# Experts' weight stream reordered: the next expert's first up pair is projected between an expert's last pair and its down projection

## The reference, cut to what matters

```python
def swiglu(t, w1, w3, w2):
    return (jax.nn.silu(t @ w1) * (t @ w3)) @ w2

def moe_swiglu(h, w_router, b_router, w1, w3, w2):
    shp = h.shape
    t = h.reshape(-1, shp[-1])
    logits = (t @ w_router).astype(jnp.float32) + b_router.astype(jnp.float32)
    top_v, top_i = lax.top_k(logits, TOP_K)          # TOP_K = 2
    top_w = jax.nn.softmax(top_v, axis=-1)
    combine = jnp.sum(jax.nn.one_hot(top_i, N_EXPERTS, dtype=jnp.float32) * top_w[..., None], axis=1)
    y = None
    for e in range(N_EXPERTS):                       # 8
        ye = combine[:, e:e + 1] * swiglu(t, w1[e], w3[e], w2[e]).astype(jnp.float32)
        y = ye if y is None else y + ye
    return y.astype(h.dtype).reshape(shp)
```

## Time and profile before

| | |
|---|---|
| Median of three runs | 2604.79 us |
| Profiled execution | 2603.11 us |
| Its span | 2601.3 us |
| Mean granted TensorE clock | 0.962 |
| TensorE matmuls busy | 2434.9 us, 94% of the span |
| VectorE, ScalarE, GpSimd busy | 1768.2, 1260.9, 525.7 us |
| HBM read | 500.33 MB |
| Experts' stage | about 1785 to 2584 us of the span |

### The profile page before, as it was taken

The page is one execution under the profiler, slowest core; times in us unless marked ns, Lnnn a source line. Parts: engine busy times, 40 slices in busy tenths (PEclk is TensorE's granted clock), DMA queues, the critical chain, the costliest instruction groups (busy, mean ns, idle before and its releaser), DMA issues.

```text
span 2601.3 us, 36325 instructions
## 1 busy us (share of the span) xinstructions
PE 2434.9 (94%) x13800; PEld 2037.3 (78%) x13824; DVE 1768.2 (68%) x1887; ACT 1260.9 (48%) x1457; POOL 525.7 (20%) x407
## 2 busy tenths in 40 slices
PE   7999999999999988779999989889999999999997
PEld 5668998769997855658889967577788888887886
DVE  6566865456865766558645357657888888888886
ACT  5444344444433455332222134536667677677674
POOL 1003531003522000031002520002142232222321
PEclk9989999999999998789999989888999999999999
DMA  5424554454552310025555323026989889889894
GB/s 195 161 82 155 179 185 159 175 196 151 189 195 77 114 41 1 33 88 193 192 193 192 130 73 115 9 84 228 347 321 365 336 336 352 335 343 357 324 363 181
DMA packets 71469, 503.73 MB, mean 194 GB/s; under 512 B 8193, under 2 KB 8705, under 8 KB 11265
## 3 DMA queue, kind: packets, MB, share of 16 engines
q1 hardware_dynamic: 70128, 496.75, 52.0%
q0 software_dynamic: 1168, 4.66, 0.5%
HBM read 500.33 MB, written 1.05 MB: 193 GB/s over the span
## 4 chain that ended last, share of the span: by engine, by line
PE 83%; DVE 10%; ACT 4%; issue 2%; POOL 1%; DMA 0%; DVEq 0%; ACTq 0%; SPq 0%; PEldq 0%
PE ps L418 80%; DVE ring_r L2103 1%; DVE h L2081 1%; PE ps L458 1%; POOL h_r L1350 1%; DVE h L2079 1%; DVE areaA L2073 1%; PE ps L1174 1%; ACT ring_hi L1467 1%; DVE h L2083 1%; ACT h L1546 1%; DVE areaB L2595 1%; DVE temp L2166 0%; DVE h L2680 0%; PE ps L561 0%
## 5 line engine op out<-in xcount | busy, mean ns | idle before, releaser
L1467 ACT ACTIVATE ring_hi<-ring 128x2048 fp32r<-128x2048 f32 x427 | 807.5, 1893 | 576.6 <-PE ps L418 351.1
L2852 DVE TENSOR_TENSOR ring_r<-ring,ring_hi 128x2048 fp32r<-128x2048 f32 x264 | 628.9, 2389 | 114.9 <-ACT ring_hi L1467 113.9
L418 PE MATMUL ps<-ring_hi,extra_r 128*128 128x512 f32 (+2 forms) x1808 | 610.3, 394 | 32.0 <-DVE ring_r L2103 18.4
L2103 DVE TENSOR_TENSOR ring_r<-ring,ring_hi 128x2048 fp32r<-128x2048 f32 (+3 forms) x163 | 384.6, 2359 | 197.7 <-ACT ring_hi L1467 182.9
L418 PE MATMUL ps<-extra_r,ring_hi 128*128 128x256 f32 (+1 forms) x1432 | 462.5, 323 | 21.7 <-POOL h_r L1350 20.2
L418 PE MATMUL ps<-extra_r,ring_r 128*128 128x256 f32 (+1 forms) x1432 | 458.0, 320 | 0.0
L418 PE MATMUL ps<-h_r,ring_hi 128*128 128x256 f32 (+2 forms) x1400 | 445.7, 318 | 0.0
L418 PEld LDWEIGHTS ps<-ring_hi,extra_r 128*128 128x128 f32 x1808 | 343.7, 190 | 109.1 <-DVE ring_r L2103 21.4
L418 PE MATMUL ps<-ring_r,extra_r 128*128 128x512 f32 (+2 forms) x1104 | 427.0, 387 | 0.0
L418 PEld LDWEIGHTS ps<-extra_r,ring_hi 128*128 128x128 f32 x1432 | 272.8, 190 | 45.4 <-POOL h_r L1350 23.4
L418 PEld LDWEIGHTS ps<-extra_r,ring_r 128*128 128x128 f32 x1432 | 272.7, 190 | 19.0
(11 more groups left out here) (356 smaller groups left out, 3257.0 us busy)
## 6 DMA issues: line engine op xcount, KB each, us to landing
ring<-in_experts SPq DMA_DIRECT2D x264, 1024.0 KB, 4.9
ring<-in_stream SPq DMA_DIRECT2D x202, 1024.0 KB, 4.8
ring<-in_stream SPq DMA_DIRECT2D x6, 512.0 KB, 3.6
ring<-in_stream SPq DMA_DIRECT2D x2, 576.0 KB, 3.7
res<-in_xT SPq DMA_DIRECT2D x1, 1024.0 KB, 6.0
res<-in_ctxT POOLq DMA_DIRECT2D x1, 1024.0 KB, 7.4
h<-in_consts POOLq DMA_DIRECT2D x2, 512.0 KB, 4.8
areaB<-in_cond_rows POOLq DMA_DIRECT2D x1, 1024.0 KB, 6.4
```

What stands on the lines that cost most here:

```text
L418: return pe.matmul(o, l, r, start=start, stop=stop, skip_group_check=True)
L1467: return act.activation(dst, src, ACT.Copy)
L2103: L.tell(TTN(ring_lo[:, s, 0:n], ring[:, s, 0:n], ring_hi[:, j % HIS, 0:n].bitcast(F32), ALU.subtract), "weights_lo")
L2852: TTN(ring_lo[:, s, :], ring[:, s, :], ring_hi[:, j % HIS, :].bitcast(F32), ALU.subtract).then_inc(sig("weights_lo"), 1)
```

## The change: what it does

The stream's order becomes a table, `EXPERT_ORDER`: after chunk 21 of an expert come chunks 0 and 1 of the next, then its own chunks 22 to 32, then chunk 2 of the next. TensorE's program, the order of loads, the layout of the weights in HBM and the walks of ScalarE and VectorE follow that table. The two halves of the expert's output (banks 3 and 2) are taken out by separate instructions of 512 columns: bank 3 first, then the split of a chunk, then bank 2. The waits before the down projection move inside its first chunk, whose matmuls into bank 2 go first. The waits of ScalarE and of the loads on TensorE's progress use one semaphore, `moe_used`, in place of four. VectorE's copy of gathered tokens comes before the split of its position, not after. The held-back split at position 21 stays only for the last expert.

The order table and TensorE's program:

```diff
@@ -113,6 +113,13 @@
         "n2_0": [(hf, q) for q in range(4) for hf in range(2)], "n1_1": ONE + [(1, q) for q in range(4)],
         "n2_1": ONE, "final": ONE}
 ROUTED = 80
+EXPERT_ORDER = [(0, 0), (0, 1)]
+for _e in range(NE):
+    EXPERT_ORDER += [(_e, _c) for _c in range(2, KF)]
+    if _e < NE - 1:
+        EXPERT_ORDER += [(_e + 1, 0), (_e + 1, 1)]
+    EXPERT_ORDER += [(_e, _c) for _c in range(KF, CPE)]
+EXPERT_AT = {x: _n for _n, x in enumerate(EXPERT_ORDER)}
 MIXED = {"even": 0, "odd": 2, "mix0": 4, "mix1": 8}
...
@@ -1225,28 +1224,48 @@
     pe.wait_ge(sig("xexp_hi"), i * (2 * NE) + 1)
     gather_share(0, 0)
     pe.wait_ge(sig("wcur"), i * (2 * NE) + 2)
+    def up(e, j):
+
+        n = e * NP + j
+        b = n % 2
+        if j == 0:
+            pe.wait_ge(sig("xexp_hi"), i * (2 * NE) + (2 * e + 2))
+            pe.wait_ge(sig("xexp"), i * (2 * NE) + (2 * e + 2))
+        pe.wait_ge(sig("moe_val"), i * (NE * NP) + (n + 1))
+        for half in range(2):
+            v = expert_weights(i, EXPERT_AT[e, 2 * j + half], "p (k c) -> p k c", k=4)
+            for k4 in range(4):
+                k = 4 * half + k4
+                m = mm3(ps[:, b, :], lambda s: xexp[s][:, e % 2, k, :], lambda s: v[s][:, k4, :],
+                        k == 0, k == KD - 1)
+            m.then_inc(sig("moe_used"), 1)
+
+    def down(e):
+
+        for c in range(KF // 2):
+            v = expert_weights(i, EXPERT_AT[e, KF + c], "p (k c) -> p k c", k=2)
+            pe.wait_ge(sig("moe_hidden"), i * (NE * NP) + (e * NP + c + 3))
+            steps = [(kk, a) for a in range(2) for kk in range(2)] if c == 0 else [
+                (kk, a) for kk in range(2) for a in range(2)]
+            for x, (kk, a) in enumerate(steps):
+                kt = 2 * c + kk
+                if c == 0 and x == 2:
+                    pe.wait_ge(sig("moe_turned"), i * (NE * NP) + (e * NP + NP + 1))
+                m = mm3(ps[:, 2 + a, :], lambda s: hid[s][:, kt, :],
+                        lambda s: v[s][:, kk, a * 512:(a + 1) * 512], kt == 0, kt == KF - 1)
+            m.then_inc(sig("moe_used"), 1)
+
+    up(0, 0)
     for e in range(NE):
 
-        pe.wait_ge(sig("xexp_hi"), i * (2 * NE) + (2 * e + 2))
-        pe.wait_ge(sig("xexp"), i * (2 * NE) + (2 * e + 2))
-        for j in range(NP):
+        for j in range(1, NP):
             n = e * NP + j
-            b = n % 2
-
-            pe.wait_ge(sig("moe_val"), i * (NE * NP) + (n + 1))
-            for half in range(2):
-                v = expert_weights(i, e * CPE + 2 * j + half, "p (k c) -> p k c", k=4)
-                for k4 in range(4):
-                    k = 4 * half + k4
-                    m = mm3(ps[:, b, :], lambda s: xexp[s][:, e % 2, k, :], lambda s: v[s][:, k4, :],
-                            k == 0, k == KD - 1)
-                m.then_inc(sig("moe_half") if half == 0 else sig(f"moe_up{b}"), 1)
+            up(e, j)
             if j == 1 and e:
-
-                pe.wait_ge(sig("yexp"), i * NE + e)
-            if j:
-                turn_pair(i, n - 1)
+                pe.wait_ge(sig("yexp"), i * (2 * NE) + (2 * e - 1))
+            turn_pair(i, n - 1)
             if j == 3 and e:
+                pe.wait_ge(sig("yexp"), i * (2 * NE) + 2 * e)
                 scatter(e - 1)
             if e == NE - 1:
                 continue
...
+        if e < NE - 1:
+            up(e + 1, 0)
         turn_pair(i, e * NP + NP - 1)
-
-        if e < NE - 1:
-            pe.wait_ge(sig("xexp"), i * (2 * NE) + (2 * e + 4))
-        pe.wait_ge(sig("moe_turned"), i * (NE * NP) + (e * NP + NP + 1))
...
+        down(e)
+
+    pe.wait_ge(sig("yexp"), i * (2 * NE) + 2 * NE)
     scatter(NE - 1).then_inc(sig("scattered"), 1)
```

SyncE's wait for a free slot, and ScalarE's walk:

```diff
-    sem, value, per = moe["plan"][n - SLOTS][2]
-    sp.wait_ge(sem, i * (per // 2) + value)
+    sp.wait_ge(sig("moe_used"), i * GROUP + (n - SLOTS + 1 + HIS))
     sp.sem_inc(sig("slot_open"), 1)
...
+    act.wait_ge(sig("moe_used"), i * (NE * CPE) + (n + 1))
     copy(ring_hi[:, (moe["split"] + n) % HIS, :], ring[:, s, :]).then_inc(sig("weights_hi"), 1)
...
+    for p, (e, c) in enumerate(EXPERT_ORDER):
+        leaving = c == 2 and e > 0
+        if leaving:
             act.wait_ge(sig("wcur"), i * (2 * NE) + 2 * e)
-            act.wait_ge(sig("moe_down"), i * (NE * KF // 2) + (HIS + e * (KF // 2)))
-            expert_out(e - 1)
...
+            consumed(e - 1, CPE - 1)
+            expert_out(e - 1, 1)
+        if c == KF and e == NE - 1:
+            turned(i, e * NP + NP - 1)
+        if p + 2 < NE * CPE:
+            expert_hi(i, p + 2)
+        if leaving:
+            expert_out(e - 1, 0)
...
+        consumed(e, c)
+
+        act.wait_ge(sig("moe_val"), i * (NE * NP) + (n + 1))
+        act.activation(msil[:, b, :], ps[:, b, 0:NM], ACT.Silu).then_inc(sig("moe_silu"), 1)
+        if n:
+            turned(i, n - 1)
...
+    consumed(NE - 1, CPE - 1)
+    for a in (1, 0):
+        expert_out(NE - 1, a)
```

VectorE's walk:

```diff
+def expert_out(i, e, a):
+
+    dve.wait_ge(sig("yexp_hi"), i * (2 * NE) + (2 * e + 2 - a))
+    STT(out=yexp[1][:, 512 * a:512 * a + 512], in0=ps[:, 2 + a, :], scalar=wcur[:, e % 2:e % 2 + 1],
+        in1=yexp[0][:, 512 * a:512 * a + 512].bitcast(F32), op0=ALU.mult,
+        op1=ALU.subtract).then_inc(sig("yexp"), 1)
...
+    for p, (e, c) in enumerate(EXPERT_ORDER):
+        leaving = c == 2 and e > 0
+        late = c == KF - 1 and e == NE - 1
+        if leaving:
             dve.wait_ge(sig("wcur"), i * (2 * NE) + 2 * e)
-            dve.wait_ge(sig("yexp_hi"), i * NE + e)
-            expert_out(e - 1)
-        if e == NE - 1:
+            expert_out(i, e - 1, 1)
+        if c == 2 and e == NE - 1:
...
+        if c in (16, 20) and e < NE - 1:
+            dve.wait_ge(sig("gather_full"), i * (5 * NE) + (5 * e + 8 + 2 * (c == 20)))
+            gathered(1 - e % 2, int(c == 20), 2)
+        if p + 2 < NE * CPE and not late:
+            expert_lo(i, p + 2)
+        if leaving:
+            expert_out(i, e - 1, 0)
...
+        b = n % 2
+
+        dve.wait_ge(sig("moe_silu"), i * (NE * NP) + (n + 1))
+        TTN(mprod[:, b, :], ps[:, b, NM:2 * NM], msil[:, b, :], ALU.mult).then_inc(sig("moe_val"), 1)
+        if late:
+            expert_lo(i, p + 2)
     dve.wait_ge(sig("wcur"), i * (2 * NE) + 2 * NE)
```

More of the change, by code:

```diff
@@ L1187, in _ @@
             for n in range(NE * CPE):
-                e, c = divmod(n, CPE)
                 s = (len(chunks) + n) % SLOTS
                 loads[s] += 16
[L1191 to L1198, removed]
+                plan.append((s, loads[s]))
             per_slot = [b - a for a, b in zip(slot_loads, loads)]
@@ L1202, in _ @@
             for _ in range(HIS):
[L1203 removed]
+                pe.sem_inc(sig("moe_used"), 1)
             def expert_weights(i, n, pattern, **dims):
@@ L1306, in load_expert @@
             def load_expert(group, n):
-                e, c = divmod(n, CPE)
                 slot = moe["plan"][n][0]
-                sp.dma_start(ring[:, slot, :], A["experts"][group * (NE // 2) + e, c, :, :]).then_inc(slot_full[slot], 16)
+                sp.dma_start(ring[:, slot, :], A["experts"][group, n, :, :]).then_inc(slot_full[slot], 16)
             def opened(i, n):
-                sem, value, per = moe["plan"][n - SLOTS][2]
-                sp.wait_ge(sem, i * (per // 2) + value)
+                sp.wait_ge(sig("moe_used"), i * GROUP + (n - SLOTS + 1 + HIS))
                 sp.sem_inc(sig("slot_open"), 1)
@@ new lines, in _ @@
+                        consumed(e - 1, CPE - 1)
[6 more added lines that the diff above has]
+                        expert_out(e - 1, 0)
+                    if c in (14, 18) and e < NE - 1:
+                        act.wait_ge(sig("gather_full"), i * (5 * NE) + (5 * e + 7 + 2 * (c == 18)))
+                        gathered(1 - e % 2, int(c == 18), 2)
@@ L2878, in _ @@
                         dve.wait_ge(sig("rank"), i + 1)
-                    for c in range(CPE):
-                        if e * CPE + c + 2 < NE * CPE and c != KF - 1:
-                            expert_lo(i, e * CPE + c + 2)
-                        if c == 6:
-                            picks((e + 1) % NE)
-                        if c == 12 and e < NE - 1:
-                            dve.wait_ge(sig("gather_full"), i * (5 * NE) + (5 * e + 6))
-                            gathered_share(1 - e % 2, 2)
-                        if c in (16, 20) and e < NE - 1:
-                            dve.wait_ge(sig("gather_full"), i * (5 * NE) + (5 * e + 8 + 2 * (c == 20)))
-                            gathered(1 - e % 2, int(c == 20), 2)
-                        if c >= KF or c % 2 == 0:
-                            continue
-                        n = e * NP + c // 2
-                        b = n % 2
-                        dve.wait_ge(sig("moe_silu"), i * (NE * NP) + (n + 1))
-                        TTN(mprod[:, b, :], ps[:, b, NM:2 * NM], msil[:, b, :], ALU.mult).then_inc(sig("moe_val"), 1)
-                        if c == KF - 1:
```

(16 more changed lines are left out.)

55 lines of the change are left out of this document (12 added, 43 removed).

## The result

The changed kernel takes 2590.86 us (median of six runs, 2590.34 to 2593.62), the kernel before 2604.88 us (median of six, 2599.67 to 2612.74): 14.0 us less, a ratio of 0.9948 with a 95% interval of 0.9934 to 0.9962. The profiled execution took 2590.83 us, its span is 2589.0 us against 2601.3, so 12.3 us of the difference are in the two traces.

What follows compares the result with a forecast made beforehand. TensorE bounds the kernel, its matmuls busy 94% of the span, so gains come from its own time or gaps. 13.9 + 0.9 + 0.4 = 15.2 us off 2603.1 gives 2587.9, 1.7 more for the median; forecast 2589.5, range 2586.5 to 2597.

Steps and rivals of the forecast that it cites:

- The boundary: At seven expert boundaries, 1.85 us less of waits for product and copy plus 0.14 of stall: 1.99 each, 13.9 in all.
- Halves of 0.60 and 0.68 us: Assumed times of the 512-column output instructions on ScalarE and VectorE, taken from the nearest rows, copies out of PSUM.
- queue walk: ScalarE's and VectorE's queues after a down projection: nothing late, VectorE's first half done at T + 2.5, tightest spare 0.4 us.
- Rounding beside GpSimd: VectorE's rests and GpSimd hold each other up at the boundary; 0.9 us spare less 0.46 leaves 0.4, so nothing charged.
- The last boundary: At the last expert the down projection no longer waits for the copy out of bank 3: gain 0.9 us.
- The tail: After the last down projection, TensorE's 2.52 us idle for the output becomes 2.1 with halves: gain 0.4 us.
- Nothing is added on TensorE: In the sum, TensorE's matmuls and transposes stay the same, so no cost is charged against the 15.2 us.
- Loads: Weight chunk loads keep number and size, their rate rises; 3.2 us spare, about 349 GB/s in the period, no stall.
- Splitting late: Rival: chunk 5 or the down projection's second chunk is late at each boundary, some 8 us, 2597; chance 0.13.
- loads: Rival: load rate cannot rise over 342 GB/s, seven periods stay at 101.3, gain only 1.3 us, 2603; chance 0.03.
- covers: Rival: the seventh matmul still waits for bank 3, up to 1.6 us back at each boundary, about 2601; chance 0.05.
- slower: Rival: bank 3 not empty at T + 5.5, each boundary costs more than it saves, 7 us slower, 2612; chance 0.04.

Runs made afterwards that it cites:

- e1: The changed kernel with the next expert's pair 0 put back behind the down projection, all else kept; median 2592.48 us, period 100.22 to 100.36 us.
- e2: The changed kernel with the whole down projection waiting for the copy out of bank 3, its first chunk alternating banks as before; median 2597.76 us, ratio 0.9977 to before.
- e5: The changed kernel with the output's halves in the other order, bank 2 first, then the split, then bank 3; one run 2599.05 us, period 99.77 us.
- e3: The changed kernel with each expert's output taken out whole, one 1024-column instruction each on ScalarE and VectorE; median 2589.66 us, period 99.39 us.
- e7: The changed kernel with silu called once on a scratch tile before the experts' loop, loading its table early; one run, 2588.71 us.

## Why the prediction was right

Forecast 2589.5 us in a range of 2586.5 to 2597, measured 2590.86; forecast a gain of 15.2 us, measured 14.0 in the medians and 12.3 in the traces. That the total came within 1.4 us is partly luck, since totals scatter by more than that; what bears the prediction out is the period, 99.39 against the 99.3 forecast, and the waits. By its steps:

- **The boundary, 1.99 us each.** Period 101.33 to 99.39, 1.94 each and 13.6 in all against 13.9. Right, and shown in its two halves by e1 (product) and e2 (copy). The pairs at 5.50 in place of 5.47, which no step had, cost 0.14 of it; the gaps themselves gave a little more than charged.
- **Halves of 0.60 and 0.68 us.** Measured 0.68 and 0.74 (means of the 14 between experts): the nearest rows were closer than half the whole or the whole. The queue walk was right to 0.2 us, and e5 found its tightest place where it lay. Half-sized instructions did not decide: e3.
- **Rounding beside GpSimd, no charge.** Right. The 264 rests take 619.7 us in place of 628.9: the two back-to-back ones at a boundary, 5.49 before, take 4.57 after (from 2248.03).
- **The last boundary, 0.9 us.** From the last turn to the first matmul of the down projection 1.10 became 0.19: 0.91, right. But the turn itself comes 0.09 later behind pair 10 (1.18 us after the turn of pair 9, 1.09 before): silu starts 0.10 behind the pair's end and not 0.02, with the short instruction that e7 is about ahead of it. So 0.82.
- **The tail, 0.4 us.** 0.3 up to the scatter: TensorE's idle time there is 2.22 in place of 2.52. But the step ended there, and the 1.83 us lost behind it, to the clock, were in no term. The clock leaving 1.00 was one of the prediction's signs of being wrong; over the experts' period it stayed at 1.00, and at the end it left it in both kernels.
- **"Nothing is added on TensorE."** True, but one place outside the boundary lost 0.55 us: the table load behind the wait for pair 0. The prediction took four semaphores made one as free on ScalarE. That step failed, at its small size, there and in the 0.09 above.
- **Loads.** 349 GB/s in the period, as worked out, 377 over a down projection, and no wait for a load. (The spare of a load was 8.3 less 4.8, that is 3.5 us; the prediction has 3.2.)
- **Rivals.** Splitting late, loads, covers and slower: the changed kernel's trace shows none. e2 shows what the cover of bank 3 was worth, 7.5 us.

From the transposes to the end the traces differ by 12.1 us, and the misses add up to that: 15.2 less 0.3 (seven boundaries), 0.1 (last boundary), 0.55 (table), 0.2 (the last expert's pairs at 5.50 in place of 5.47: from its pair 2 to its turn of pair 9 are 52.91 us, before 52.67), 0.1 (tail) and 1.8 (clock). The other 0.2 of the 12.3 lie ahead of the transposes.

## What to carry to other kernels

Where an engine that is 99% busy waits at a seam for its own product's way through two others, put a unit of independent work of the next round into the seam; before that, walk the queues behind it, since every buffer that two rounds gave time to empty now has one. Ordering the first matmuls so that those which need no wait come first was worth more here than the moved work (7.5 and 6.0 us), for no cost that a trace shows. And where a serial end follows a dense stage, read the granted clock there: beside a change of 13 us, 2 were lost in code that it does not touch.

## What the runs showed of the hardware that was not expected

- TensorE idles 2.2 to 2.7 us ahead of the last scatter. In every trace without dummies the granted clock is at the 1.2 GHz level in a part of the 10 us after it: in the scatter, in the sum of squares, or in both. In e1 and e5 the scatter still runs at 2.4 GHz (2.16 us) behind the same idle time, and the clock falls later. With 10 and 8 dummy matmuls it is 1.00 throughout, and the end is 3.1 us shorter.
- The 1.28 us load of silu's table starts 0.66 us later when the short instruction ahead of it stands behind the wait, and that cost 0.55 us.
- The 24 matmuls of a pair take 5.50 or 5.47 us, at clock 1.00, in the same kernel and in either order. This stays open.
